# A two-block, one-core kernel: first convolution tap on ScalarE, gates by features, modulation by transposes, new step orders

## The reference

```
y[t, c] = sum_j w[j, c] * x[t - 3 + j, c]        # the convolution of q, k, v: tap 3 is the token itself
mod = silu(c) @ w_ada + b_ada                    # 6 x 1024 values for all tokens
gates = hn @ w_in[:, 14 gate columns]            # 256 x 14
```

## Time and profile before

| what | value |
|---|---|
| median of three runs | 1134.78 us |
| the profiled execution, its own time | 1137.42 us |
| its span, first to last instruction | 1135.6 us |
| mean granted TensorE clock over the span | 0.981 |
| TensorE busy with matmuls | 1091.9 us, 96% |
| VectorE busy | 797.0 us, 70% |
| ScalarE busy | 617.5 us, 54% |
| GpSimd busy | 13.0 us, 1% |

### The profile page before, as it was taken

How to read it: one execution, slowest core, us unless ns; L and a number is a source line. 1 busy time by engine, 2 the same in 40 slices (tenths; PEclk the granted TensorE clock), 3 DMA queues, 4 the chain that set the end, 5 groups by cost and what they waited for, 6 DMA issues and landing times.

```text
span 1135.6 us, 18650 instructions
## 1 busy us (share of the span) xinstructions
PE 1091.9 (96%) x7532; PEld 978.7 (86%) x7532; DVE 797.0 (70%) x1084; ACT 617.5 (54%) x695; POOL 13.0 (1%) x13
## 2 busy tenths in 40 slices
PE   6999999999988999999999999999999888999998
PEld 6999999999875799989899987669986658999986
DVE  5999974787327679789797955747886556555653
ACT  5774542653233576769668643675675445444331
POOL 0100000000000000000000000002000000000000
PEclk9999999999989999999999999998999899999999
DMA  8444332335305663434333354774444055555460
GB/s 326 161 181 145 136 127 90 131 130 185 118 32 196 234 237 112 149 113 149 117 144 113 135 199 151 293 315 156 143 147 182 20 187 194 179 180 178 167 214 19
DMA packets 26292, 181.29 MB, mean 160 GB/s; under 512 B 3040, under 2 KB 3296, under 8 KB 4960
## 3 DMA queue, kind: packets, MB, share of 16 engines
q1 hardware_dynamic: 25056, 174.66, 42.3%
q10 hardware_dynamic: 1152, 5.45, 1.3%
HBM read 179.04 MB, written 1.05 MB: 159 GB/s over the span
## 4 chain that ended last, share of the span: by engine, by line
PE 82%; DVE 7%; ACT 7%; issue 2%; DMA 1%; POOL 0%; ACTq 0%; SPq 0%; DVEq 0%; POOLq 0%
PE PS L922 80%; ACT WH L1368 2%; DVE WL L1800 2%; ACT L1735 1%; PE PS L1075 1%; DMA layer<-xt 1%; PE PS L1291 1%; DVE PS L1768 0%; DVE YL L1812 0%; DMA RAW<-wst 0%; PE PS L1153 0%; DVE layer_ln L2128 0%; POOL layer L2358 0%; DVE layer L2105 0%; ACT layer L1378 0%
## 5 line engine op out<-in xcount | busy, mean ns | idle before, releaser
L922 PE MATMUL PS<-XTH,WH 128*128 128x256 f32 x1392 | 406.9, 292 | 3.8 <-DVE XTL L2017 3.8
L922 PE MATMUL PS<-XTL,WH 128*128 128x256 f32 x1392 | 397.1, 285 | 0.0
L922 PE MATMUL PS<-XTH,WL 128*128 128x256 f32 x1392 | 396.9, 285 | 0.0
L1800 DVE TENSOR_TENSOR WL<-RAW,WH 128x2048 fp32r<-128x2048 f32 x138 | 316.7, 2295 | 113.1 <-ACT WH L1368 110.6
L1368 ACT ACTIVATE WH<-RAW 128x2048 fp32r<-128x2048 f32 x138 | 262.6, 1903 | 211.0 <-PE PS L922 207.0
L922 PEld LDWEIGHTS PS<-XTH,WH 128*128 128x128 f32 x1392 | 270.6, 194 | 7.0 <-ACT XTH L1525 4.6
L922 PEld LDWEIGHTS PS<-XTL,WH 128*128 128x128 f32 x1392 | 270.6, 194 | 2.4 <-issue 2.4
L922 PEld LDWEIGHTS PS<-XTH,WL 128*128 128x128 f32 x1392 | 270.3, 194 | 0.0
L922 PE MATMUL PS<-WH,YH 128*128 128x512 f32 x224 | 90.7, 405 | 3.7 <-DVE YL L1812 2.6
L1735 ACT ACT_TABLE_LOAD x71 | 91.1, 1283 | 1.7 <-ACT norms L1533 0.3
L922 PE MATMUL PS<-WH,YL 128*128 128x512 f32 x224 | 87.9, 393 | 0.0
(11 more groups left out here) (294 smaller groups left out, 1284.8 us busy)
## 6 DMA issues: line engine op xcount, KB each, us to landing
RAW<-wst SPq DMA_DIRECT2D x162, 1024.0 KB, 4.9
LNW<-lnrow ACTq DMA_DIRECT2D x3, 1024.0 KB, 4.8
RAW<-wst SPq DMA_DIRECT2D x4, 512.0 KB, 4.9
layer<-xt SPq DMA_DIRECT2D x2, 512.0 KB, 5.7
...
```

The costliest lines, as they stand in the source:

```text
L922: return pe.matmul(o, lhsT, rhs, start=start, stop=stop)
L1800: tt(WL[:, i % RAW_RING, 0:n], RAW[:, i % RAW_RING, 0:n], as_float(WH[:, k % SPLIT_RING, 0:n]), ALU.subtract).then_inc(vector_done, 1)
```

## The change

1. `conv` skips the last tap for q, k and v, and a new ScalarE step `tap` writes it. VectorE's step now waits for `tap`.

```diff
+            def s_tap(kind, g, p):
+                act.wait_ge(tensor_done, tensor_at(kind, g, p))
+                act.wait_ge(vec_loaded, 16)
+                i = conv_units.index((kind, g, p))
+                if i >= 2:
+                    act.wait_ge(scalar_done, scalar_at(*conv_units[i - 2]))
+                tile = {"q": 0, "k": 8, "v": 16}[kind] + g * HG + 2 * p
+                for a in range(2):
+                    s = slice(a * T, (a + 1) * T)
+                    last = fn(CV[:, i % 2, s], PS[:, bank_of(kind, g, p), s], ACT.Copy, scale=v("conv_b", (tile + a) * 4 + 3))
+                last.then_inc(scalar_done, 1)
...
+            def conv(acc, src, weight, taps, first=True):
+                for a in range(2) if first else ():
                     last = ts(acc[:, a, :], src[:, a, :], weight(a, taps - 1), None, ALU.mult)
                 for back in range(1, taps):
-                    link(last)
+                    if first or back > 1:
+                        link(last)
...
+                    dve.wait_ge(scalar_done, scalar_at("tap", kind, g, p))
```

```diff
-                s = slice(c * P, (c + 1) * P)
-                products(PS[:, step.banks[0], 0:NG],
-                                [((XTH[:, k, s], XTL[:, k, s]), (WGH[:, k, :], WGL[:, k, :])) for k in range(KC)]).then_inc(tensor_done, 1)
+                if part:
+                    pe.wait_ge(vector_done, vector_at("gates", 0))
+                    for c in range(NT):
+                        last = pe.transpose(PS[:, step.banks[0], c * NG:(c + 1) * NG], GTR[0:NG, c * P:(c + 1) * P],
+                                            ident[0:NG, 0:NG])
+                    last.then_inc(tensor_done, 1)
+                    return
+                pe.wait_ge(vector_done, vector_at("wg2"))
+                wl, wh = ([WGW[:, (a * KC + k) * NG:(a * KC + k) * NG + P] for k in range(KC)] for a in range(2))
+                products(PS[:, step.banks[0], 0:T], [((wh[k], wl[k]), x_tile(k)) for k in range(KC)]).then_inc(tensor_done, 1)
...
+            def v_wg2():
+                n = KC * NG
+                dve.tensor_copy(WGW[:, 0:n], as_float(flat(WGL[:])))
+                dve.tensor_copy(WGW[:, n:2 * n], as_float(flat(WGH[:])))
+                ts(WGW[:, 2 * n:2 * n + P], ONES[:], 0.0, None, ALU.mult).then_inc(vector_done, 1)
```

```diff
-                    last = mm(PS[:, step.banks[0], j:j + 1], MROW[:, j * P:(j + 1) * P], ONES[:, 0:1])
+                    last = pe.transpose(PS[:, step.banks[0], j * P:(j + 1) * P], MROW[:, j * P:(j + 1) * P], ident)
...
-                tt(MODT[:, r, o:o + 4], PS[:, b, 0:4], v("bada", r * KC + o, 4), ALU.add).then_inc(vector_done, 1)
+                parts4 = PS[:, b, :].rearrange("p (j a n) -> p j a n", j=4, a=4)[:, :, :, 0]
+                link(dve.tensor_reduce(MODT[:, r, o:o + 4], parts4, AX.X, ALU.add))
+                tt(MODT[:, r, o:o + 4], MODT[:, r, o:o + 4], v("bada", r * KC + o, 4), ALU.add).then_inc(vector_done, 1)
```

```diff
+            for _ in range(6):
+                mm(PS[:, 7, :], ONES[:], ONES[:].unsqueeze(1).to_broadcast([P, 4, P]))
```

```diff
-            at[0] += (4 * int(np.prod(shape[1:])) + 31) // 32 * 32
+            at[0] += (4 * int(np.prod(shape[1:])) + 63) // 64 * 64
```

6. `ORDER_T` (499 steps), `ORDER_S` (423 steps, then 435) and `ORDER_V` (523, then 524) are written anew. Five places, shown as the words of the lists. The start of TensorE and of VectorE:

```diff
-ba first:k:0:0 k:0:0 first:k:0:1 k:0:1 first:v:0:0 v:0:0 norm:k:0
+first:k:0:0 ba k:0:0 first:k:0:1 k:0:1 first:v:0:0 v:0:0 norm:k:0
...
-setup xs:0 xs:1 split_top split:0:0 split:1:1 ba split:2:2 k:0:0 split:3:3 k:0:1 split:4:4 v:0:0 split:5:5 norm:k:0 split:6:6 ba1 q:0:0 ba2
+xs:0 split_top xs:1 split:0:0 split:1:1 split:2:2 ba ba1 k:0:0 split:3:3 k:0:1 ba2 setup split:4:4 v:0:0 norm:k:0
```

The end of layer 0's second group of heads on TensorE; `out:0:0:2` and `out:0:1:2` stood among levels 2 and 3 before:

```diff
-gv:1:0 gu:1:6:1 gs:1 gks:1 gv:1:1 go:1 gr:1:0 gr:1:1 pl:0:0 first:out:0:0:3 first:out:0:1:3
+gv:1:0 gx:1:5:1 gs:1 gu:1:6:1 gks:1 out:0:0:2 gv:1:1 go:1 gr:1:0 pl:0:0 gr:1:1 out:0:1:2 first:out:0:1:3 first:out:0:0:3
```

The attention heads of block 2: `val:1:1` stood before `turn:3`, `gm` before `score:0` on ScalarE, `ada:5` after `score:7`:

```diff
+turn:3 score:5 score:6 turn:4 pv:2 pv:3 score:7 score:8 turn:5 val:1:1 turn:6 ... turn:11 ada:5:0 ada:5:1 pv:10 pv:11 adat:4 turn:12
+split:101:123 pv:1 gm turn:3 score:5 pv:3
```

VectorE before the MLP:

```diff
-rmsb:1:1 adat:10 split:106:132 xt:5:1 xt:5:3 xtl:5:2 xtl:5:0 xtl:5:3 xtl:5:1 adat:11 split:107:133
+rmsb:1:1 split:106:132 xt:5:3 xtl:5:0 xt:5:1 xtl:5:1 xtl:5:2 adat:10 adat:11 xtl:5:3 split:108:134
```

More of the change, by code:

```diff
@@ L275, in conv, with unit_and_tap @@
     def conv(name, g):
-        return pair(name, g, on="TVS", readers="V")
+        def unit_and_tap(p):
+            unit(name, g, p, on="TVS", slab=(name, g, p), readers="V")
+            step("tap", name, g, p, on="S")
+        return [later(unit_and_tap, p) for p in range(2)]
     def gdn(g):
@@ L410, in plan @@
     ada(4)[0]()
-    for c in range(NT):
-        unit("gates", c, on="TV")
+    step("wg2", on="V")
+    unit("gates", 0, on="TV")
+    unit("gates", 1, on="TV")
     feat(8)
@@ L504 @@
-out:1:0:3 out:1:1:3 xt:2:0:0 pl:1:1 ada:8:0 xt:2:0:1 ada:8:1 ada:6:0 xt:2:1:0 ada:6:1 adat:8 xt:2:1:1 first:gate:1:0:0
-first:gate:1:0:1 gate:1:0:0 gate:1:0:1 first:gate:1:1:0 adat:6 first:gate:1:1:1 gate:1:1:0 gate:1:1:1 ada:7:0 ada:7:1
-ada:9:0 ada:9:1 xt:4:2 xt:4:0 xt:4:3 ada:4:0 xt:4:1 adat:7 adat:9 ada:4:1 gates:1 gates:0 first:feat:8 feat:8 gcol
-first:feat:0 qn:1:2 feat:0 first:feat:1 qn:0:0 feat:1 first:feat:2 qn:0:1 feat:2 first:feat:3 qn:0:2 feat:3
-first:feat:4 grow:0 feat:4 first:feat:5 feat:5 grow:1 first:feat:6 feat:6 first:feat:7 qn:1:0 feat:7 first:val:0:0
@@ new lines @@
+first:z1:3:1 i:3:1 hm:3:3 hm:3:2 z1:3:1 ada:3:0 ada:3:1 out:1:0:0 hm:3:4 adat:3 hm:3:5 out:1:1:0 hm:3:6 hc:3 out:1:0:1
+ho:3 out:1:1:1 hr:3:0 hr:3:1 out:1:0:2 pl:1:0 out:1:1:2 first:out:1:1:3 first:out:1:0:3 out:1:0:3 out:1:1:3 xt:2:0:0
+pl:1:1 ada:8:0 ada:8:1 xt:2:0:1 ada:6:0 xt:2:1:0 xt:2:1:1 ada:6:1 adat:8 first:gate:1:0:0 first:gate:1:0:1 gate:1:0:0
+gate:1:0:1 first:gate:1:1:0 adat:6 first:gate:1:1:1 gate:1:1:0 gate:1:1:1 ada:7:0 ada:7:1 ada:9:0 ada:9:1 ada:4:0
+xt:4:0 adat:7 xt:4:3 xt:4:2 xt:4:1 adat:9 ada:4:1 gates:0 first:feat:8 gates:1 feat:8 first:feat:0 qn:1:2 feat:0
@@ new lines @@
+split:72:79 split:73:80 hz:2 split:74:81 hy:3:0 hd:3 hx:3:2 hr:2:0 split:75:82 hy:3:1 hy:3:2 hp:3:0 hx:3:3 hx:3:4
+hy:3:3 hx:3:5 hp:3:1 split:76:85 hp:3:2 hy:3:4 hy:3:5 hx:3:7 hp:3:3 split:77:86 adat:3 split:78:87 hx:3:6 hp:3:4
+hp:3:5 hy:3:6 hy:3:7 hp:3:6 split:79:88 split:80:89 hz:3 split:82:91 split:81:90 hr:3:0 split:83:92 hr:3:1
+first:out:1:1:3 first:out:1:0:3 lna:1:0 lnb:1:0:0 out:1:0:3 out:1:1:3 lna:1:1 xt:2:0:0 lnb:1:0:1 lnb:1:1:0 lnb:1:1:1
+split:84:98 xt:2:0:1 xt:2:1:0 split:85:99 wg2 mod:0 adat:8 split:86:100 xt:2:1:1 first:gate:1:0:1 split:87:101
@@ new lines @@
+gate:1:0:1 adat:6 first:gate:1:1:1 rmsb:0:0 gate:1:1:1 rmsb:0:1 xt:4:3 adat:7 xt:4:1 xtl:4:0 xtl:4:2 xtl:4:3 xtl:4:1
+split:88:108 gates:0 split:89:109 gates:1 ga gb adat:9 gd split:90:110 qn:1:2 split:91:111 qn:0:0 split:92:112
+split:93:113 gsp split:94:114 qn:0:1 gcol qn:0:2 split:95:115 feat:3 grow:0 split:96:116 feat:4 grow:1 split:97:117
+qn:1:0 split:98:118 score:0 mb qn:1:1 ratio:0 score:1 split:99:119 ratio:1 score:2 split:100:120 ratio:2 score:3
+score:4 gm ratio:3 ratio:4 split:101:123 pv:1 score:5 score:6 ratio:5 score:7 ratio:6 pv:3 score:8 ratio:7 ratio:8
@@ L597 @@
+split:117:143 ff:10 ff:11 split:119:145 split:120:146 ff:13 ff:12 split:121:147 split:122:148 split:123:149 ff:14
+split:124:150 ff:15 split:125:151 ff:16 split:126:152 ff:17 ff:19 ff:18 split:127:153 split:128:154 split:129:155
+ff:20 ff:21 split:130:156 split:131:157 split:133:159 split:132:158 split:134:160 first:down:0:5 split:135:161
+split:136:162 split:137:163 split:138:164 down:0:5 first:down:1:5 down:1:5
 """
```

228 lines of the change are left out of this document (108 added, 120 removed).

## The result

The changed kernel takes 1101.45 us (median; 1100.44 to 1103.03) against 1134.09 (1133.07 to 1135.26) for the kernel before on the same chip: a ratio of 0.9713, interval 0.9696 to 0.973. The gain is 32.6 us. The forecast was 16.9, and its range ended at 1105: the prediction had the sign right and the size half.

A forecast was written before the change was run, and what follows sets the result against it. TensorE was taken as the bound, busy 1091.9 of 1135.6 us. Terms 3.5 + 0.6 (GpSimd's gt:0 wait) + 6.0 + 1.5 + 5.5 + 2.3 + 1.5 - 4 = 16.9 off the median of 1134.8 gave 1118 us; range 1105 to 1130.

The forecast's parts named there:

- Start: First 24 us: six added matmuls raise the clock before k:0:0 and ba moves; gain 3.5 us, from 5.8 lost to 4.5 gained.
- The tap: Convolution taps of q, k, v moved from VectorE to ScalarE: costed at nothing, as cover letting the start's gain last.
- rival D: Taps behind ScalarE's WH copies hold VectorE's conv, the next split and TensorE: slower, 1147 us; chance 0.05.
- Gates: Gates around first:feat:8: 24 matmuls and two transposes replace 48 matmuls at low clock; gain 6.0 us, 4.1 to 7.9.
- adat: Eight modulation rows spread by 32 transposes instead of products with ones; gain 1.5 us, none to 2.9.
- Homes: Tiles placed at 64-byte addresses: worth nothing, 1 us either way.
- Before the MLP: TensorE's 3.78 us idle for xtl:5:0 shrinks as VectorE loses work ahead of it; gain 2.3 us, bounds 1 and 3.
- End of layer 0's recurrence: 325 to 347.3 us: two sets of 24 wide matmuls cover pauses and keep the clock; gain 5.5, 9 gained to 2 lost.
- Heads: 880 to 917 us: val:1:1 covers pauses and half clock, gm's exponentials join ScalarE; gain 1.5 us, bounds 5 either way.
- The other reordered steps: Some 1400 other steps whose new order brings its own TensorE pauses: 4 us taken back, 0 to 15.
- rival C: Whole kernel: new orders take nothing back and the clock holds at 325 and 880 us; 1107 us, chance 0.11.
- TensorE's busy time below 1080 us: Sign listed to show the forecast: TensorE's busy time over the whole kernel under 1080 us, from 1091.9 before.

The follow-up runs named there:

- experiment 5: Changed kernel without the six matmuls of ones at the start: 1104.35 us, ratio 0.9718 to the kernel before.
- experiment 4: Changed kernel with the first convolution tap back on VectorE, in all its new sequences: 1104.31 us, ratio 0.9734 to the kernel before.
- 1: The changed kernel's operations in the step sequences of the kernel before, only the new steps inserted: 1144.73 us, ratio 1.0078 to the kernel before.
- 2: The changed kernel's operations except the tap, which stays on VectorE, in the step sequences of the kernel before: 1130.12 us, ratio 0.9949 to the kernel before.
- experiment 6: Changed kernel with the gates as before (x stationary, 14 columns moving, 48 matmuls, both ahead of first:feat:8): 1108.21 us, ratio 0.9765 to the kernel before.
- 11: Changed kernel with all three engines' sequences of feature stage and heads (ada:4:1 to pv:15) put back to the old order: 1118.65 us, ratio 0.9851 to the kernel before.
- experiment 7: Changed kernel with out:0:0:2 and out:0:1:2, and their slabs' splits, put back among levels 3 and 4 of the recurrence: 1110.48 us, ratio 0.9781 to the kernel before.
- 12: Kernel before, operations unchanged, with the changed kernel's three sequences from ada:4:1 to pv:15 (feature stage and heads): 1122.89 us, ratio 0.9913 to the kernel before.
- experiment 8: Changed kernel with neighbouring pv and score pairs in the heads set apart, in TensorE's order alone: 1110.7 us, ratio 0.9783 to the kernel before.
- 13: Changed kernel with all three sequences of layer 1's four recurrence groups (hf:0 to hc:3) put back to the old order: 1097.12 us, ratio 0.9658 to the kernel before.

## Why the prediction was wrong, step by step

*Start, 3.5 us.* Right. The twelve records ended at 9.5 us (10 forecast), the first weight matmul came at 9.49 ("near 10"), k:0:0 was done at 19.06 (19.7). The timeline after, to the earlier trace rows:

```profile
1.06 8.46 PE L929 MATMUL PS<-ONES 128*128 128x512 f32 x12 [1.06 <-POOL EPS L2391]
...
12.45 3.64 PE L929 MATMUL PS<-WBA,layer 128*128 128x16 f32 x32
```

4.8 us were had at its end; 3.1 are left at gc:0, where `gt:0` is no longer waited for, and the six matmuls are worth 2.9 by experiment 5.

*The tap, nothing.* The duration was right (0.471 us), and so was the verdict on the rule of the Trainium skill (Trainium Architecture — The Big Picture, The five engines, in one table): at 128 x 256 out of PSUM ScalarE is level with VectorE's 0.479, not 3 times slower. The effect was not nothing. In the sequences that came with it it gives 2.9 us (experiment 4); in the old ones, with the taps where I put them, it costs 14.6 (1 against 2), by the mechanism of rival D, through another queue neighbour than the one I named: not behind a `WH` copy, but behind ScalarE's norm steps. I took the new order's answer to this for granted without counting it as part of the edit.

*Gates, 6.0.* Right in mechanism and size: 6.8 (experiment 6). I had priced a badly placed copy at 0.5 us; in the old order it costs 2.9, because the next slab's split stands behind it (11). *adat, 1.5*: 2.4, within its bounds. *Homes, 0*: 0. *Before the MLP, 2.3*: 2.9; the pause before ff:0 is 1.30 us, under the 1.8 I set:

```profile
907.50 0.35 PE L929 MATMUL PS<-XTH,WH 128*128 128x256 f32 x1 [1.30 <-ACT XTH L1553]
```

*End of layer 0's recurrence, 5.5.* Right mechanism, too small: 9.0 by experiment 7, which I had as the far bound, and 8.2 by the table above. Part of it is a slip: the terms that I added from 332.3 come to 350.0 and not to 351.0, a gain of 6.5. I had expected VectorE's slabs 37 to 39 to be late behind the chain; none of them is, nor is the last output slab, which waited 1.53 us before. The clock did the rest: 1.00 instead of 0.85.

*Heads, 1.5 (5 either way).* **This is the step that failed.** By the step ends it is 11.3 us, and the order of this stretch and the one before it is worth 11.9 us in the kernel before and 17.2 in the changed one (11, 12). I had priced the heads by their pauses and half clock alone (5.2 and 3.3 us), and looked for what the new order would do to those. That left each product at a constant duration, whatever stands beside it. It isn't constant: 8.0 us of the 11.3 are the same 148 records in 20.3 instead of 28.3 us. Overlap of neighbours makes some 4.5 us: seven pairs that the old order does not have, three of `score` at 0.8 and four of `pv` at 0.52, the prices that experiment 8 has shown at full clock. The clock is up to 3.4 more: before, it is at half from 894.8 to 901.7 us, and after never in this stretch. The pauses fell too, from 4.9 us (67.0 - 62.15 in the window from 849 to 916 of before) to 2.5. What is left, about 1 us, was not taken apart; fewer changes of shape may be in it. So the pauses and the clock, which I had on my rows, gave more than my 1.5 as well, up to 5.8. The bound of 5 for the whole term was taken from the pauses, and so could not hold it. What should have made me look was in the trace of before: two `score` steps that ended 0.01 us apart at 128 x 384 of output.

*The other reordered steps, -4 (0 to 15 lost).* The sign holds in one place: layer 1 loses 5.0 us, and 4.3 are had back by its old order (13). Elsewhere the reordering gains, 3.6 us between gc:0 and level 3, and between the recurrence and the gates outside layer 1 some 2 beyond the 2.5 of the seven `adat` rows there, in part where the clock no longer falls. This term was given as one number for 1400 steps without a view that could carry it. In sum it was +0.4 rather than -4.

Between the two profiled executions the gain is 35.7 us, so that the sum of 16.9 misses 18.8 (15.7 by the medians). By the table above the heads make 9.8 of it, the end of the recurrence 2.7 and this last term 4.4; the rest is the gates, the `adat` rows and the stretch before the MLP, less what the start fell short of. The chances had rival C at 1107 as the best case: it held the clock, and not the overlap. My sign for "TensorE's busy time below 1080 us" was met by far (1067.3), and I had not asked how 1400 steps in a new order could make TensorE's busy time fall. The trace has a second answer beside overlap: the kernel before is at half clock for 3.4 us each at 171, 369, 724 and 943 us, which no term of mine priced and which the changed kernel does not have.
